# The even layer takes its latent tokens by grid column; its neighbourhood heads score 512 keys in place of 768

## The reference

```
rs   = clip(row - kh // 2, 0, rows - kh)        # kh = 8 = rows, so rs = 0
cs   = clip(col - 8, 0, 64 - 16)
kcol = cs + arange(16);  krow = rs + arange(8)
s_nb  = q . k[krow, kcol] + rpb[krow - row + 7, kcol - col + 15]
s_ctx = q . k_ctx
p = softmax(concat([s_nb, s_ctx]));  out = p @ concat([v_nb, v_ctx])
```

## Time and profile before

| what | us |
|---|---|
| median of 3 runs | 2598.48 |
| the profiled execution's own time | 2600.93 |
| its span | 2599.1 |
| PE busy | 2405.3 (93%) |
| DVE busy | 1625.2 (63%) |
| ACT busy | 974.8 (38%) |
| POOL busy | 365.9 (14%) |
| attention of layer 1, from its first scores | 1037.39 to 1245.65 |
| its neighbourhood half, from the first latent scores | 1142.58 to 1245.65 |

### The profile page before, as it was taken

The page is one execution under the profiler, slowest core; times in us unless marked ns, Lnnn a source line. Parts: engine busy times, 40 slices in busy tenths (PEclk is TensorE's granted clock), DMA queues, the critical chain, the costliest instruction groups (busy, mean ns, idle before and its releaser), DMA issues.

```text
span 2599.1 us, 33349 instructions
## 1 busy us (share of the span) xinstructions
PE 2405.3 (93%) x13242; PEld 1928.7 (74%) x13242; DVE 1625.2 (63%) x2761; ACT 974.8 (38%) x1768; POOL 365.9 (14%) x355
## 2 busy tenths in 40 slices
PE   7988998999989899998989999999979898999996
PEld 3865567888878777565768888888867676888875
DVE  3448676565765641888767765656464885765455
ACT  4335453322212421666343231322332773423232
POOL 0110103010021100000300123123141000000123
PEclk9999999999999899999989999999989999999998
DMA  6231125554443221100311332333122103332321
GB/s 238 92 102 49 33 66 191 206 179 137 159 150 121 98 68 52 58 30 15 132 55 65 130 114 97 106 121 115 57 89 66 42 2 128 132 113 81 106 90 49
DMA packets 79002, 255.48 MB, mean 98 GB/s; under 512 B 5632, under 2 KB 10368, under 8 KB 70400
## 3 DMA queue, kind: packets, MB, share of 16 engines
q1 hardware_dynamic: 65024, 203.44, 22.6%
q0 software_dynamic: 12528, 45.62, 5.1%
q10 hardware_dynamic: 1296, 4.30, 0.4%
HBM read 243.89 MB, written 9.44 MB: 97 GB/s over the span
## 4 chain that ended last, share of the span: by engine, by line
PE 69%; DVE 14%; ACT 6%; issue 4%; POOL 1%; DMA 0%; DVEq 0%; POOLq 0%; ACTq 0%
PE PS L975 9%; PE PS L977 9%; PE PS L976 9%; PE PS L1011 5%; PE PS L1012 5%; PE PS L1013 5%; PE PS L746 3%; PE PS L743 3%; PE PS L744 3%; PE PS L843 3%; PE PS L856 2%; PE PS L885 2%; PE PS L952 2%; ACT HT L2216 2%; PE PS L950 2%
## 5 line engine op out<-in xcount | busy, mean ns | idle before, releaser
L975 PE MATMUL PS<-HH,WH 128*128 128x512 f32 x1056 | 417.8, 396 | 7.6 <-DVE WL L1836 5.9
L976 PE MATMUL PS<-HL,WH 128*128 128x512 f32 x1056 | 414.6, 393 | 0.0
L977 PE MATMUL PS<-HH,WL 128*128 128x512 f32 x1056 | 414.3, 392 | 0.0
L2079 ACT ACTIVATE WH<-STG 128x1024 fp32r<-128x1024 f32 (+1 forms) x204 | 198.9, 1023 | 304.9 <-PE PS L1013 240.2
L1836 DVE TENSOR_TENSOR WL<-STG,WH 128x1024 fp32r<-128x1024 f32 (+1 forms) x204 | 239.3, 1214 | 47.5 <-ACT WH L2079 47.3
L1011 PE MATMUL PS<-WH,AH 128*128 128x512 f32 x616 | 246.0, 399 | 13.4 <-DVE WL L1836 5.0
L1012 PE MATMUL PS<-WL,AH 128*128 128x512 f32 x616 | 244.2, 396 | 0.0
L1013 PE MATMUL PS<-WH,AL 128*128 128x512 f32 x616 | 243.8, 396 | 0.0
L975 PEld LDWEIGHTS PS<-HH,WH 128*128 128x128 f32 x1056 | 200.8, 190 | 50.8 <-issue 7.5
L976 PEld LDWEIGHTS PS<-HL,WH 128*128 128x128 f32 x1056 | 200.8, 190 | 42.2 <-issue 1.0
L977 PEld LDWEIGHTS PS<-HH,WL 128*128 128x128 f32 x1056 | 200.5, 190 | 42.3
(11 more groups left out here) (213 smaller groups left out, 4365.6 us busy)
## 6 DMA issues: line engine op xcount, KB each, us to landing
STG<-in_w_up SPq DMA_DIRECT2D x66, 1024.0 KB, 6.9
ADAW<-in_w_ada SPq DMA_DIRECT2D x96, 512.0 KB, 4.0
STG<-in_w_down SPq DMA_DIRECT2D x20, 1024.0 KB, 5.1
ADAW<-in_w_ada POOLq DMA_DIRECT2D x32, 512.0 KB, 4.2
STG<-in_w_ffn_out SPq DMA_DIRECT2D x10, 1024.0 KB, 7.1
STG<-in_ev_w_in SPq DMA_DIRECT2D x8, 1024.0 KB, 5.1
spill<-X POOLq DMA_DIRECT2D x14, 512.0 KB, 4.9
STG<-in_w_in SPq DMA_DIRECT2D x6, 1024.0 KB, 5.5
```

The source lines that it names most:

```text
L975: e.matmul(PS[:, b, 0:T], h_, HH[gi][:, c, :], start=first, stop=False)
L976: e.matmul(PS[:, b, 0:T], h_, HL[gi][:, c, :], start=False, stop=False)
L977: return e.matmul(PS[:, b, 0:T], l_, HH[gi][:, c, :], start=False, stop=last)
```

## The change

The layer's latents are permuted to column order (token' = 8 * column + row) where `turn_x` of layer 1 writes the transposed input (`turned_in`, `turned_from`: the write steps by 8 elements), so that a latent tile is 16 whole columns of the grid. The outputs are permuted back where ACT copies an item's output from PSUM to X (`attended`, `attention_out`: read by steps of 8 elements, written in runs of 16 into all four latent tiles); this holds for the latent items of both halves. RoPE of layer 1 uses tables in column order: POOL loads them over the old ones in the feed-forward stage of layer 0, and loads the old ones again in that of layer 1.

A latent tile of queries in the neighbourhood half now needs at most 256 latent keys, so an item scores 512: the context and two tiles' worth of latents. Tiles 2 and 5 do it with two pieces of 256 a head; tiles 3 and 4 with four pieces (256, 64, 64, 128), as their neighbourhood is half a tile to either side. The values to these two halves are put together in `LOW` by four copies of 64 x 512 on POOL (`VC`), and the first output of the attention waits for the last of them. The bias tables get zeros for the context and have 1280 columns (640 KB); one `lowest` over 512 columns is left for each head. Head 1's table moves: it is loaded when the last global scores are done, as are those of heads 2 and 3.

The diff, without the declaration of a semaphore and the entry that feeds the table:

```diff
@@ -329,6 +330,33 @@
+    def turned_in(self, L, vec, c, n):
+        v = self.turn_place(L, c, n)
+        return v.rearrange("p (c r) -> p r c", r=8) if (L, vec) == (1, 0) else v
+    def turned_from(self, L, vec, c, n):
+        v = self.ps(("xt", L, vec, c))[:, 0:n]
+        return v.rearrange("p (r c) -> p r c", r=8) if (L, vec) == (1, 0) else v
+    def rope_table(self, L):
+        return self.rope_in(L) if L else self.con_in()
+    def attended(self, L, it):
+        x = slice(it["col"] * P, (it["col"] + 1) * P)
+        if L != 1 or it["tt"] < 2:
+            return self.x(it["tt"])[:, x]
+        i = it["tt"] - 2
+        v = self.X[:, 2048:6144].rearrange("p (j w) -> p j w", j=4)[:, :, x]
+        return v.rearrange("p j (r c) -> p j r c", r=2)[:, :, :, 16 * i:16 * i + 16]
+    def attention_out(self, L, p, it):
+        v = self.result(L, p)
+        return v if L != 1 or it["tt"] < 2 else v.rearrange("p (c j r) -> p j r c", j=4, r=2)
     def turn_place(self, L, c, n):
@@ -587,15 +615,14 @@
-    def neighbourhood(hp):
-        for h in (2 * hp, 2 * hp + 1):
-            if hp == 1:
-                w.wait_ge(*k.pe_score((1, 23)))
-            elif hp > 1:
-                w.wait_ge(*k.dv_max((1, 2 * (24 + 6 * (hp - 2) + 5) + h % 2)))
-            o = bias_place(h)
-            e.dma_start(k.reg(1, o, o + 896), t["nb"][h]).then_inc(*k.nb_in[h % 4].up(h))
+    def neighbourhood(h):
+        if h >= 4:
+            w.wait_ge(*k.dv_max((1, 2 * (24 + 6 * (h // 2 - 2) + 5) + h % 2)))
+        elif h:
+            w.wait_ge(*k.pe_score((1, 23)))
+        o = bias_place(h)
+        e.dma_start(k.reg(1, o, o + 1280), t["nb"][h]).then_inc(*k.nb_in[h % 4].up(h))
@@ -627,8 +654,8 @@
         if L == 1:
-            for hp in range(1, 4):
-                neighbourhood(hp)
+            for h in range(1, 8):
+                neighbourhood(h)
         ffn(L, ada(11, 16) if L == 1 else ada(16, 17))
@@ -878,6 +905,8 @@
             self.free(b)
+            if self.name == 1:
+                w.wait_ge(*k.pl_table(("values", 3, 64)))
             for j in range(2):
@@ -1285,6 +1314,7 @@
     QB, KB, VB = k.reg(1, 4608, 7680, 4), k.reg(1, 7680, 10752, 4), k.reg(1, 10752, 13824, 6)
+    VC = k.LOW[:, 0:1024].rearrange("p (c t) -> p c t", c=2)
     out = []
@@ -1294,13 +1324,25 @@
                     kt = KA[64 * s:64 * s + 64, :] if part == 0 else KB[64 * s:64 * s + 64, c, :]
-                    mm.append([(0, 512, q, kt[:, 0:512]), (512, 256, q, kt[:, 512:768])] if tt >= 2 else
-                              [(0, 256, q, kt[:, 0:256])])
+                    ctx = [(0, 256, q, kt[:, 0:256])]
+                    if tt < 2:
+                        mm.append(ctx)
+                    elif part == 0:
+                        mm.append([(0, 512, q, kt[:, 0:512]), (512, 256, q, kt[:, 512:768])])
+                    elif tt == 2:
+                        mm.append([(0, 256, q, kt[:, 256:512]), (256, 256, q, kt[:, 0:256])])
+                    elif tt == 5:
+                        mm.append(ctx + [(256, 256, q, kt[:, 512:768])])
+                    else:
+                        mm.append(ctx + [(256, 64, q, kt[:, (tt + 1) * P:(tt + 1) * P + 64]), (320, 64, q, kt[:, tt * P - 64:tt * P]),
+                                         (384, P, q, kt[:, tt * P:(tt + 1) * P])])
                     if part == 0:
                         vs.append(lambda i, s=s: VA[:, i, s * 64:(s + 1) * 64])
+                    elif tt in (3, 4):
+                        vs.append(lambda i, h=h, tt=tt: (VB[:, i] if i < 2 else VC[:, tt - 3] if i == 2 else VB[:, tt])[:, h * 64:(h + 1) * 64])
                     else:
-                        vs.append(lambda i, h=h: VB[:, i, h * 64:(h + 1) * 64])
-                nk = 768 if tt >= 2 else 256
+                        vs.append(lambda i, h=h, tt=tt: VB[:, i if tt < 2 else (i + 2) % 4 if tt == 2 else i + i // 2 * 2, h * 64:(h + 1) * 64])
+                nk = (768, 512)[part] if tt >= 2 else 256
                 out.append({"mm": mm, "v": vs, "nk": nk, "nkt": nk // P, "tt": tt, "col": 4 * part + hp,
@@ -1350,7 +1392,12 @@
-    return 13824 + h % 4 * 896 if h % 4 < 2 else (h % 4 - 2) * 896
+    return 13824 if h % 4 == 0 else (h % 4 - 1) * 1280
+def bias_columns(tt):
+    return {2: 0, 3: 256, 4: 256, 5: 768}[tt]
@@ -1479,7 +1526,7 @@
                     w.wait_ge(*k.dv_htl((L, 1 - vec, c + 4)))
-                e.tensor_scalar(k.turn_place(L, c, n), k.ps(("xt", L, vec, c))[:, 0:n], sc[:, c:c + 1], sh[:, c:c + 1],
+                e.tensor_scalar(k.turned_in(L, vec, c, n), k.turned_from(L, vec, c, n), sc[:, c:c + 1], sh[:, c:c + 1],
                                 ALU.mult, ALU.add).then_inc(*k.dv_ht.up((L, vec, c)))
@@ -1502,7 +1549,7 @@
         sn = sn.rearrange("p (f g) -> p f g", f=4)
-        w.wait_ge(*k.con_in())
+        w.wait_ge(*k.rope_table(key[0] if key[0] in (1, 2) else 0))
         e.tensor_tensor(heads(t1, n), src, bc_mid(cs, n), ALU.mult)
@@ -1704,13 +1751,10 @@
                 if it["bias"]:
-                    h, y0, first = it["bias"][j], 6 - 2 * (it["tt"] - 2), k.small("att", n, 3)
-                    o = bias_place(h) + 64 * y0
-                    w.wait_ge(*k.pl_table("zero"))
-                    lowest(S[:, 0:256], k.LOW[:, 0:256], -NEG, first).then_inc(*k.dv_bias.up((L, n)))
-                    w.wait_ge(*k.dv_bias((L, n)))
+                    h = it["bias"][j]
+                    o = bias_place(h) + bias_columns(it["tt"])
                     w.wait_ge(*k.nb_in[h % 4](h))
-                    lowest(S[:, 256:768], k.reg(1, o, o + 512), first, low).then_inc(*k.dv_max.up((L, n)))
+                    lowest(S[:, 0:512], k.reg(1, o, o + 512), -NEG, low).then_inc(*k.dv_max.up((L, n)))
                 elif "sink" in it:
@@ -2113,7 +2157,7 @@
                     w.wait_ge(*k.dv_htl((L, 1 - vec, c + 4)))
-                e.activation(k.turn_place(L, c, n), k.ps(("xt", L, vec, c))[:, 0:n], ACT.Identity, bias=sh[:, c:c + 1],
+                e.activation(k.turned_in(L, vec, c, n), k.turned_from(L, vec, c, n), ACT.Identity, bias=sh[:, c:c + 1],
                              scale=sc[:, c:c + 1]).then_inc(*k.ac_ht.up((L, vec, c)))
@@ -2240,7 +2284,10 @@
             w.wait_ge(*k.pe_out((name, p)))
-            copy(k.x(it["tt"])[:, it["col"] * P:(it["col"] + 1) * P], k.result(name, p)).then_inc(*k.ac_out.up((name, p)))
+            if L == 0:
+                copy(k.x(it["tt"])[:, it["col"] * P:(it["col"] + 1) * P], k.result(name, p)).then_inc(*k.ac_out.up((name, p)))
+            else:
+                copy(k.attended(L, it), k.attention_out(L, p, it)).then_inc(*k.ac_out.up((name, p)))
@@ -2651,6 +2698,8 @@
         if L < 2:
+            a, b = KK["cos"][0], KK["sin"][1]
+            e.dma_start(k.CON[:, a:b], t["rope1"] if L == 0 else t["con"][:, a:b]).then_inc(*k.rope_in.up(L + 1))
             for v in range(2 if L == 0 else 1):
@@ -2744,7 +2793,16 @@
         if L == 1:
-            e.memset(k.LOW[:, 0:256], 0.0).then_inc(*k.pl_table.up("zero"))
+            w.wait_ge(*k.ac_plain((1, 28)))
+            w.wait_ge(*k.dv_bank((1, 29)))
+            VB = value_view(k, 1, "vb")
+            last = None
+            for i in range(2):
+                for r, tt in ((slice(0, 64), i + 4), (slice(64, P), i + 2)):
+                    if last:
+                        w.wait_ge(*k.pl_table(last))
+                    last = ("values", tt, r.start)
+                    e.tensor_copy(k.LOW[r, 512 * i:512 * i + 512], VB[r, tt, :]).then_inc(*k.pl_table.up(last))
         for v in range(2 if L == 1 else 1):
@@ -2831,15 +2889,25 @@
-    col, x = np.arange(64)[:, None], np.arange(64)[None]
-    first = np.clip(col - 8, 0, 48)
-    inside = (x >= first) & (x < first + 16)
-    d = np.clip(x - col + 15, 0, 30)
-    out = np.empty((8, 2, 64, 14, 64), rpb.dtype)
-    for r in range(2):
-        rows = rpb[:, 1 - r:15 - r][:, :, d].transpose(0, 2, 1, 3)
-        out[:, r] = np.where(inside[None, :, None, :], rows, np.asarray(NEG, rpb.dtype))
-    return out.reshape(8, P, 896)
+    out = np.zeros((8, P, 5, 256), rpb.dtype)
+    i = np.arange(P)
+    for n, (tile, pieces) in enumerate(((0, (0, 128)), (1, (256, 64, 128)), (3, (256, 384)))):
+        keys = np.concatenate([a + np.arange(64 if n == 1 and a != 128 else 128) for a in pieces])
+        qc, qr = 16 * tile + i[:, None] // 8, i[:, None] % 8
+        kc, kr = keys[None] // 8, keys[None] % 8
+        first = np.clip(qc - 8, 0, 48)
+        inside = (kc >= first) & (kc < first + 16)
+        v = rpb[:, kr - qr + 7, np.clip(kc - qc + 15, 0, 30)]
+        out[:, :, 2 * n] = np.where(inside[None], v, np.asarray(NEG, rpb.dtype))
+    return out.reshape(8, P, 1280)
+def rope_by_column(con):
+    a, b = KK["cos"][0], KK["sin"][1]
+    v = con[:, a:b].reshape(P, 2, 4, 64).transpose(1, 2, 0, 3).reshape(2, 8, 64, 64)
+    return v.transpose(0, 2, 1, 3).reshape(2, 4, P, 64).transpose(2, 0, 1, 3).reshape(P, b - a)
```

(2 more changed lines are left out.)

## The result

The changed kernel takes **2576.78 us** (median, 2576.01 to 2577.09), against 2598.64 (2597.49 to 2601.83) for the kernel before, run beside it: a ratio of 0.9913, 95% interval 0.9896 to 0.9931. That is 21.9 us less; forecast were 25.2 less and 2573.3 us. The profiled execution took 2576.80 us, its span is 2575.0. Against the profile before that is 24.1 less, and I compare profiles with profiles here.

A forecast was written before the change was run, and what follows sets the result against it. PE leads, with each neighbourhood item costing its scores plus the longer of PE's own work or the chain. Gains of 27.5 us less 1.0, 1.0 and 0.25 give 25.2, so 2573.3 us; range 2564 to 2583.

The forecast's parts named there:

- the chain minimum, exponential, output copy: Neighbourhood half, DVE's minimum to ACT's output copy, releasing PE's next scores: 2.71 us behind a context item, forecast 2.05.
- C: First latent item of a neighbourhood group (tile 2), from scores to scores: 4.20 us before, forecast 3.12.
- D and E: Latent items of tiles 3 and 4 in a neighbourhood group: 5.05 and 4.89 us before, forecast 3.36 each.
- F: Latent item of tile 5 in a neighbourhood group, from scores to scores: 4.88 us before, forecast 3.33.
- A: First context tile of the next pair of heads: 4.00 us before, forecast 3.43, including a stall of 0.55.
- B: Second context tile of the next pair of heads: 2.93 us before, forecast 2.49 through a shorter output.
- the tail: Neighbourhood half, from the last scores to the last output's end: 11.09 us before, forecast 8.5.
- Output copies that permute: ACT's output copies reading by steps of 32 bytes: 0.05 us more on 19 items, 1.0 us (0 to 5.1).
- The slower rival: ACT's permuting output copy takes 1.5 us in place of 0.27 and becomes the bound: 2605 us; chance 3%.
- The permuting writes: Stepped writes of `turn_x` in layer 1, four on ACT and four on DVE: 1.0 us lost (0 to 2.2).
- stepped access is dear: Rival: 32-byte steps cost four times the normal rate in `turn_x` and the output copies: 2584 us; chance 12%.
- PE alone: Rival: in the neighbourhood half only PE's own work binds, a group taking 16.9 us: 2565 us; chance 8%.

The follow-up runs named there:

- e3: The changed kernel with column order kept but neighbourhood items scoring all 768 keys, with one minimum over 768 columns; 0.9982 of the kernel before.
- e4: The changed kernel with the minimum over 512 columns done in two halves of 256; 0.9911 of the kernel before.
- e6: The changed kernel with the heads of a short item taking PSUM banks 6 and 7 in turn, not bank 6 alone; 0.9899 of the kernel before.
- e2: The changed kernel with the input's permutation made by stepped PSUM reads and SBUF written in order; 0.9895 of the kernel before.
- e7: The changed kernel with stepped PSUM reads for the input, three score pieces for tiles 3 and 4, and two banks in turn; 2571.52 us, 0.9887 of before.

## Why the prediction was right, point by point

- **What bounds the kernel.** Right. e3 and e4 separate the two parts as told: PE's own work holds most items, the chain minimum, exponential, output copy holds C.
- **The items.** C 2.98 for 3.12, D and E 3.47 and 3.50 for 3.36, F 3.40 for 3.33, A 3.39 for 3.43, B 2.71 for 2.49; the tail 8.64 for 8.5. The half gained 26.1 where 27.5 was forecast. Three groups at 0.36 us too much are 1.1 of the missing 1.4. Within a group errors cancel: the scores of D and E take 0.40 too much and B 0.22, while C takes 0.14 less, and what follows the scores in D and E 2.17 and 2.20 for 2.26.
- **The four pieces.** The mis-sized term: 1.30 for 1.10, beyond my bound of 1.17. Two steps of it failed. I took half of 1.07 for the 256 columns, as if the start of a scores block could be divided: at 0.42 for 256 columns (1.49 less 1.07), 1.07 is 0.84 of columns and 0.23 of start, and the start is paid whole. And I put the pieces of 64 just above columns alone, where each costs what one of 128 does, 0.21. Start 0.23, one piece at 0.42 and three at 0.21 give 1.28, against 1.30 measured.
- **The chain behind C.** 1.91 from the end of the scores (1147.69) to the next (1149.60), for 2.05. It was the surer of the two, being made of rows.
- **The single bank.** The stall at A was foreseen (0.53 for 0.55). I missed the same wait at D (0.19), the one at F (0.16) and the delay in B. In e6 B comes to 2.48, where 2.49 was forecast, and D stays at 3.48.
- **Output copies that permute.** 0 in place of 1.0. The copies read PSUM by steps of 32 bytes at the same 0.27 to 0.28 us as the others, and the global half takes 105.20 in e2, which has them all, against 105.19 before. The slower rival, which rested on this copy, had no ground.
- **The permuting writes.** 1.9 in place of 1.0 (e2: 1.85), within 0 to 2.2, but part of it on a path that the sum doesn't have: 1.5 are the longer writes that PE waits for, the way that was forecast, and 0.4 net are clock (0.9 lost in the projections, 0.5 less in the global half). That 1.9 lies within the bounds is partly luck. The rival "stepped access is dear" was half true: a DVE write of 512 columns takes 1.22 against 0.81, so 0.41 is added to the 0.54 that I gave its columns, 1.8 times the rate and not four times.
- **POOL, tables, RoPE.** No wait in the trace, as forecast: POOL's copies are done 6.5 us before the first output. POOL copies 64x512 in 0.65 us. The 0.25 for RoPE lies outside the stretch, and no run separates it.
- **PE alone.** Not reached: 17.83 of 19.45 is PE's. Even e7 keeps 3.4 us of waits for the output copy.
- **The sum.** -27.5 + 1.0 + 1.0 + 0.25 = -25.2 was forecast. Measured in the stretch: -26.1, -0.5, +1.5, +0.9, which is -24.2. It is this near in part because errors cancel: the half gave 1.4 too little and the writes cost 0.9 too much, while 1.0 for the output copies and the 0.25 were not needed. The rest of the distance between 2573.3 and 2576.78 is that the profile of the kernel before lay 2.45 us above its median, and that of the changed kernel on it.

The Trainium skill, "Advanced Engine Details and Errata", SBUF Cachelines, says that accesses which go to a different line each time are penalised. The stepped SBUF writes agree (0.41 us more on DVE, 0.50 on ACT for 512 columns). The section PSUM Cachelines asks for every two consecutive elements to be contiguous, and names matmuls as what suffers otherwise. The stepped PSUM reads of DVE and ACT in e2 and of the output copies show no penalty, and the measurement decides for them; no run here has a matmul on such a pattern.

What stays open: why the stepped writes bring one more stretch at 1.2 GHz, and whether the weight loads are what holds the pieces of 64.

## What to carry to other kernels

Price a block of small matmuls as one start, which can't be divided, plus its columns, and count a piece of 64 columns as one of 128. When a shorter operand makes two buffers fit one bank, keep using both banks in turn: here the single bank ate 3.4 us of a 26 us gain. Look at the clock of the stages behind the one that was changed: here they added 0.4 us to the 1.5 of the stepped writes. Where a permutation must be made on the way from PSUM to SBUF, step the read and write in order.

## What the runs showed of the hardware

- A float32 write to SBUF by steps of 32 bytes took 1.22 us in place of 0.81 on DVE and 1.28 in place of 0.78 on ACT, for 512 columns. Reads from PSUM by steps of 32 bytes (ACT, 128 columns, 0.276 against 0.275) and of 256 bytes (512 columns, 0.81 on DVE and 0.78 on ACT) took what plain ones take.
- A float32 matmul piece of 64 columns cost two heads 0.21 us, as much as one of 128 (512 keys with none, one and two such pieces a head: 1.07, 1.18, 1.30); a further piece of 128 cost its columns alone (1.07 to 1.28).
- With the stepped writes PE had one more stretch of 3.4 us at 1.2 GHz, some 60 us behind them, in six profiles of six, and in none of the four without them.
- The same work of PE ahead of layer 1 ended at 865.5 to 868.6 us in ten profiles, so a difference of 3 us between two whole executions says nothing by itself; a stretch between two landmarks around the change was additive to 0.1 us.
